# Layer 0's first four rows normed and turned two by two in all eight banks; angles at the beginning; first two pieces by halves in turns

## The reference, cut to what matters

```python
def rms_norm(x, g):
    y = x * lax.rsqrt(jnp.mean(x * x, axis=-1, keepdims=True) + NORM_EPS)
    return y * g

def partial_rope(x, pos):                 # the first 16 of 64 columns of each head
    inv = jnp.power(ROPE_THETA, -jnp.arange(half) / half)
    ang = pos[..., None] * inv
    x1, x2, rest = x[..., :half], x[..., half:ROT_DIM], x[..., ROT_DIM:]
    return concatenate([x1 * cos(ang) - x2 * sin(ang), x2 * cos(ang) + x1 * sin(ang), rest])

def swa_sink_mixer(h, pos, w_in, sinks):
    q, k, v, gate = split_cols(h @ w_in, [1024, 256, 256, 1024])
    q, k = partial_rope(q, pos), partial_rope(k, pos)
    o = banded_attention(q, k, v, SWA_WINDOW - 1, sinks)
    return o * silu(gate)

for i in range(2):
    x = x + mixer(rms_norm(x, norm)) @ w_out
return rms_norm(x, final_norm)
```

## Time and profile before

| | us |
|---|---|
| median of 3 runs | 1314.26 (1313.46 to 1314.52) |
| profiled execution, its own time | 1312.6 |
| its span | 1310.8 |
| PE busy | 1269.5 (97%) |
| DVE busy | 766.0 (58%) |
| ACT busy | 643.1 (49%) |
| POOL busy | 367.4 (28%) |

### The profile page before, as it was taken

One profiled execution on the slowest core, in us unless ns is written; L12 is line 12 of the kernel. 1 busy time (PEld: TensorE's weight loads), 2 busy tenths in 40 slices (PEclk: granted clock), 3 DMA queues, 4 the chain that ended last, 5 costly groups with the idle time before them and its releaser, 6 DMA issues. The chain is left out here.

```text
span 1310.8 us, 24577 instructions
## 1 busy us (share of the span) xinstructions
PE 1269.5 (97%) x8714; PEld 1183.4 (90%) x8714; DVE 766.0 (58%) x2339; ACT 643.1 (49%) x1777; POOL 367.4 (28%) x427
## 2 busy tenths in 40 slices
PE   4999999999899999999999999999999999998997
PEld 4998998988699999999989999899999899987997
DVE  5745453554672545666546766556765476767925
ACT  6444454454651444554446554446554455545312
POOL 2312142240301022212214932216832118611010
PEclk9999999999999999999999999999999999999999
DMA  5101012031545201110112211202310213215623
GB/s 201 38 20 50 26 54 84 18 98 38 173 146 201 97 25 53 39 26 20 53 53 67 84 57 36 65 28 81 107 34 19 65 40 100 76 27 154 192 99 129
DMA packets 101224, 97.29 MB, mean 74 GB/s; under 512 B 30705, under 2 KB 87537, under 8 KB 101105
## 3 DMA queue, kind: packets, MB, share of 16 engines
q1 hardware_dynamic: 101104, 95.73, 24.5%
HBM read 79.46 MB, written 16.25 MB: 73 GB/s over the span
## 5 line engine op out<-in xcount | busy, mean ns | idle before, releaser
L1161 PE MATMUL j_bank<-w_hi,ht_hi 128*128 128x384 f32 (+1 forms) x1312 | 445.4, 339 | 6.3 <-ACT v L1417 2.4
L1161 PE MATMUL j_bank<-w_lo,ht_hi 128*128 128x384 f32 (+1 forms) x1312 | 433.2, 330 | 0.0
L1161 PE MATMUL j_bank<-w_hi,ht_lo 128*128 128x384 f32 (+1 forms) x1312 | 433.1, 330 | 0.0
L1161 PEld LDWEIGHTS j_bank<-w_hi,ht_hi 128*128 128x128 f32 x1312 | 248.8, 190 | 18.8 <-issue 12.2
L1056 POOL TENSOR_TENSOR w_lo<-w_raw,w_hi 128x768 fp32r<-128x768 f32 (+1 forms) x60 | 103.2, 1720 | 558.6 <-ACT w_hi L1394 510.3
L1403 ACT ACTIVATE probs<-probs,stat 128x256 f32<-128x256 f32 (+1 forms) x512 | 231.2, 454 | 49.1 <-DVE stat L1661 47.5
L1161 PEld LDWEIGHTS j_bank<-w_lo,ht_hi 128*128 128x128 f32 x1312 | 249.1, 190 | 0.0
L1161 PEld LDWEIGHTS j_bank<-w_hi,ht_lo 128*128 128x128 f32 x1312 | 248.7, 190 | 0.0
L792 ACT COPY probs_t<-t_bank 128x256 f32<-128x256 f32 (+1 forms) x128 | 58.0, 453 | 289.4 <-PE o_bank L1304 283.7
L1394 ACT ACTIVATE w_hi<-w_raw 128x768 fp32r<-128x768 f32 (+1 forms) x120 | 88.6, 765 | 82.0 <-PE j_bank L1161 43.3
L1653 DVE CUSTOM_DVE_ANT_0 probs<-s_bank,masks 128x256 f32<-128x256 f32 x224 | 86.2, 421 | 54.2 <-PE t_bank L1283 53.5
(11 more groups left out here) (170 smaller groups left out, 1853.0 us busy)
## 6 DMA issues: line engine op xcount, KB each, us to landing
w_raw<-in_w_qkv SPq DMA_DIRECT2D x64, 384.0 KB, 3.4
coef<-coef_dram SPq DMA_DIRECT2D x96, 128.0 KB, 2.9
w_raw<-in_w_gate SPq DMA_DIRECT2D x32, 256.0 KB, 3.4
mix_dram<-xr SPq DMA_DIRECT2D x12, 512.0 KB, 3.9
w_raw<-in_w_out SPq DMA_DIRECT2D x16, 384.0 KB, 3.8
qk<-mix_dram SPq DMA_DIRECT2D x12, 512.0 KB, 4.2
xr<-in_x SPq DMA_DIRECT2D x8, 512.0 KB, 7.6
out<-xr SPq DMA_DIRECT2D x7, 512.0 KB, 2.7
```

The source lines that it names most:

```text
L1161: last = pe.matmul(to, a(x_, kt), b(y_, kt), start=(start and kt == kts[0] and x_ == y_), stop=(stop and kt == kts[-1] and x_ == 1))
```

## The change

The first four rows are squared one by one on ACT as they land. Rows 0 and 1 have their own `inverse` (on semaphores `first_v`, `first_a`) and are scaled on DVE; rows 2 and 3 have a second one and are scaled by DVE in columns 0 to 511 and by ACT in 512 to 1023. PE turns row 0 for all `kt`, then row 1, then rows 2 and 3 `kt` by `kt`, into eight banks at once (`first_bank`: both `j_bank`, both `t_bank` and the four of `norm_bank`). ACT calls a tiny square root first of all. Its two splits of quarters 2 and 3 stand together behind `kt` 4. PE then does half of piece 0, half of piece 1, the other half of 0, the other half of 1. The turns of rows 4 to 7 stand behind pieces 2 and 3, four `kt` each. The positions are loaded by ACT's DMA queue on their own semaphore; ACT's first `empty_norm` now waits for 32 of `small_in` (gain and sinks). `rope_angles` is cut in three: cast, products and first reduction come first of all on DVE, the second reduction stands at k = 2, and `rope_tables` moves from k = 4 to k = 3.

```diff
-NORM_BEHIND = {1: (0, 1, 2), 2: (3, 4, 5), 3: (6, 7)}
+NORM_BEHIND = [{2: (0, 1, 2, 3), 3: (4, 5, 6, 7)}, {1: (0, 1, 2), 2: (3, 4, 5), 3: (6, 7)}]
...
+        first_bank = [j_bank[PIECE.bank(("qkv", 0, 0))], j_bank[PIECE.bank(("qkv", 0, 1))], t_bank[0], t_bank[1]] + norm_bank
...
-            sp.dma_start(pos_i[:, :, :], positions).then_inc(small_in, 16)
...
+            def norm_first():
+
+                for b, e in ((0, "v"), (1, "v")):
+                    pe.wait_ge(xn_done[e], b + 1)
+                    for kt in range(KT):
+                        pe.transpose(first_bank[kt][:, b * P:(b + 1) * P], xr[:, b, kt * P:(kt + 1) * P], ident[:, :])
+                for kt in range(KT):
+                    if kt == 0:
+                        pe.wait_ge(xn_done["v"], 3)
+                    if kt == 4:
+                        pe.wait_ge(xn_done["a"], 1)
+                    for b in (2, 3):
+                        last = pe.transpose(first_bank[kt][:, b * P:(b + 1) * P], xr[:, b, kt * P:(kt + 1) * P], ident[:, :])
+                    last.then_inc(norm_full, 1)
...
             pe.wait_ge(consts, 1)
-            for kt in range(6):
-                norm_piece(0, kt, 0)
+            norm_first()
             piece(("qkv", 0, 0), (0,))
-            for kt in range(6, KT):
-                norm_piece(0, kt, 0)
+            piece(("qkv", 0, 1), (0,))
...
-                            piece(item[1:], (1,) if layer == 0 and k == 0 else (0, 1))
-                    for kt in NORM_BEHIND.get(k, ()):
+                            piece(item[1:], (1,) if layer == 0 and k < 2 else (0, 1))
+                    for kt in NORM_BEHIND[layer].get(k, ()):
...
+            act.dma_start(pos_i[:, :, :], positions).then_inc(pos_in, 16)
...
                 if layer == 0 and i == 0:
-                    act.wait_ge(small_in, 48)
+                    act.wait_ge(small_in, 32)
...
-            norm_half(0, 0, [(0, 0)])
-            w_hi([(0, 1)])
+            def square_first(n):
+
+                act.wait_ge(x_in[n], 16)
+                if n > 0:
+                    act.wait_ge(squared["va"[n % 2]], (n + 1) // 2)
+                act.activation(square_a, xr[:, n, :], ACT.Square, accum_out=sums[:, n:n + 1]).then_inc(squared["av"[n % 2]], 1)
...
+            act.activation(sums[:, NB:NB + 1], no_sink[:, 0:1], ACT.Sqrt, scale=0.0)
+            square_first(0)
+            square_first(1)
+            act.wait_ge(first_v, 1)
+            act.activation(ssq[:, 1, 0:2], ssq[:, 0, 0:2], ACT.Sqrt).then_inc(first_a, 1)
+            square_first(2)
+            square_first(3)
+            act.wait_ge(norm_v, 1)
+            act.activation(ssq[:, 1, 2:4], ssq[:, 0, 2:4], ACT.Sqrt).then_inc(norm_a, 1)
+            w_hi([(0, 0), (0, 1)])
+            act.wait_ge(norm_v, NORM_LINKS)
+            for n in (2, 3):
+                last = act.activation(xr[:, n, 512:], xr[:, n, 512:], ACT.Copy, scale=ssq[:, 2, n:n + 1])
+            last.then_inc(xn_done["a"], 1)
             for kt in range(KT):
                 empty_norm(0, kt, 0)
-                if kt == 3 or kt == 5:
-                    w_hi([(0, 2 if kt == 3 else 3)])
+                if kt == 4:
+                    w_hi([(0, 2), (0, 3)])
             norm_half(0, 1)
             w_hi(splits_of("start, next job"))
...
-            norm_half(0, 0)
+            angles()
+            less_turns(0, 2 * np.pi * 256)
+            dve.wait_ge(squared["a"], 1)
+            dve.wait_ge(squared["v"], 1)
+            inverse(0, slice(0, 2), first_v, first_a)
+            for n in (0, 1):
+                dve.tensor_scalar(xr[:, n, :], xr[:, n, :], ssq[:, 2, n:n + 1], None, ALU.mult).then_inc(xn_done["v"], 1)
+            dve.wait_ge(squared["a"], 2)
+            dve.wait_ge(squared["v"], 2)
+            inverse(0, slice(2, 4))
+            for n in (2, 3):
+                last = dve.tensor_scalar(xr[:, n, 0:512], xr[:, n, 0:512], ssq[:, 2, n:n + 1], None, ALU.mult)
+            last.then_inc(xn_done["v"], 1)
             w_lo(splits_of("start"))
             for kt in range(KT):
                 empty_norm(0, kt, 0)
-                if kt == 3:
+                if kt == 4:
                     w_lo(splits_of("start, second half"))
             norm_half(0, 1)
...
                     if layer == 0 and k == 2:
-                        rope_angles()
+                        less_turns(1, 2 * np.pi)
+                        within_half_turn()
+                    if layer == 0 and k == 3:
+                        rope_tables()
                     if layer == 0 and k == 4:
-                        rope_tables()
                         constants()
```

More of the change, by code:

```diff
@@ L523, in trunk, with bank_of_norm @@
         norm_bank = [s_bank[0], s_bank[1], o_bank[0], o_bank[1]]
+        first_bank = [j_bank[PIECE.bank(("qkv", 0, 0))], j_bank[PIECE.bank(("qkv", 0, 1))], t_bank[0], t_bank[1]] + norm_bank
+        def bank_of_norm(layer, kt, half):
+            return first_bank[kt] if layer == 0 and half == 0 else norm_bank[(KT * half + kt) % 4]
         def gate_of(layer, g):
@@ L1146, in norm_piece @@
                     pe.wait_ge(norm_empty["v"], 2 * KT * layer + i - 3)
-                elif layer == 1:
+                else:
                     pe.wait_ge(spare_empty, len(SPARE))
@@ L1150, in norm_piece @@
                     for e in "av":
-                        pe.wait_ge(xn_done[e], 4 * layer + 2 * half + 2)
+                        pe.wait_ge(xn_done[e], 4 * layer + 2 * half + (1 if e == "a" else 3))
                 for b in range(4):
@@ L1428, in empty_norm @@
                 if layer == 0 and i == 0:
-                    act.wait_ge(small_in, 48)
+                    act.wait_ge(small_in, 32)
                 if layer == 1 and kt == 0:
                     act.wait_ge(piece_full, PIECE.filled(("out", 0, OUT_PARTS - 1, 4 * half + 3)))
-                act.activation(ht[0][:, kt, half * 512:(half + 1) * 512], norm_bank[i % 4][:, :], ACT.Copy,
+                act.activation(ht[0][:, kt, half * 512:(half + 1) * 512], bank_of_norm(layer, kt, half)[:, :], ACT.Copy,
                                scale=gain[:, layer, kt:kt + 1]).then_inc(norm_empty["a"], 1)
@@ L1697, in empty_norm @@
                 dve.wait_ge(norm_empty["a"], 2 * KT * layer + i + 1)
[L1698 removed]
+                dve.scalar_tensor_tensor(out=ht[1][:, kt, cols], in0=bank_of_norm(layer, kt, half)[:, :],
                                          scalar=gain[:, layer, kt:kt + 1], in1=ht[0][:, kt, cols].bitcast(F32),
@@ L1845, in inverse_final, with inverse @@
                 inverse(4 + part, slice(*FINAL_ROWS[part]))
-            def inverse(index, blocks):
+            def inverse(index, blocks, done=norm_v, rooted=norm_a):
                 base = NORM_LINKS * index
                 var, y, z = ssq[:, 0, blocks], ssq[:, 2, blocks], ssq[:, 3, blocks]
[L1851 to L1857, removed]
+                link(dve.tensor_scalar(var, sums[:, blocks], 1.0 / D, EPS, ALU.mult, ALU.add), done, base + 1)
+                dve.wait_ge(rooted, index + 1)
+                link(dve.reciprocal(y, ssq[:, 1, blocks]), done, base + 2)
+                link(dve.tensor_tensor(z, y, y, ALU.mult), done, base + 3)
+                link(dve.tensor_tensor(z, z, var, ALU.mult), done, base + 4)
+                link(dve.tensor_scalar(z, z, -0.5, 1.5, ALU.mult, ALU.add), done, base + 5)
+                link(dve.tensor_tensor(y, y, z, ALU.mult), done, base + 6)
             def scale_rows(layer, half):
@@ L1896, in constants @@
             def constants():
+                dve.wait_ge(small_in, 32)
                 dve.tensor_scalar(neg_sink[:, :], sink[:, :], -1.0, None, ALU.mult).then_inc(sink_neg, 1)
@@ L1911, in constants, with angles @@
                 link(dve.tensor_scalar(masks[:, 5, :], key_f, row_f[:, 0:1], MASKED, ALU.is_gt, ALU.mult), mask_v, 4)
[L1913 to L1926, removed]
+            ang = rope_w[:, 0, :].rearrange("p (t j) -> p t j", j=HALF_ROT)
+            def angles():
+                dve.wait_ge(pos_in, 16)
+                link(dve.tensor_copy(pos_f[:, :, :], pos_i[:, :, :]), rope_v, 1)
                 flat = gate[:, 0, 608:608 + 3 * NB]
@@ L1930, in rope_angles, with less_turns, within_half_turn @@
                     last = dve.tensor_scalar(ang[:, :, j], flat, freq, None, ALU.mult)
-                chain(last)
+                link(last, rope_v, 2)
+            def less_turns(n, period):
+                turns, part = rope_w[:, 1, :], rope_w[:, 2, :]
                 magic = 1.5 * 2.0 ** 23
[L1933 to L1944, removed]
+                rest, parts = period, []
+                for bits in (9, 9):
+                    unit = 2.0 ** (np.floor(np.log2(rest)) - bits + 1)
+                    parts.append(np.floor(rest / unit) * unit)
+                    rest -= parts[-1]
+                parts.append(rest)
+                done = 2 + 8 * n
```

(8 more changed lines are left out.)

4 lines of the change are left out of this document (added).

## The result

| | before | after |
|---|---|---|
| median, us | 1313.47 (12 runs, 1311.94 to 1314.52) | 1315.05 (12 runs, 1313.76 to 1317.90) |
| ratio after / before | | 1.0016, 95% interval 1.0009 to 1.0024 |
| profiled execution, us | 1312.6 (span 1310.8) | 1313.8 (span 1312.0) |

The change makes the kernel slower by 1.6 us between the medians, 2.1 us by the ratio (1.2 to 3.2). The forecast was +2.2, with a time of 1316.5. Of the 1.4 us between that and 1315.05, 0.8 lies in the kernel before, whose median over 12 runs is 1313.47 and not 1314.26.

The account below looks back on a forecast made before the run. PE was taken to bound the kernel, its start settled by the wait ending at 33.10. Gains of 0.9, turns of 1.35 and a clock fall of 1.8 gave +2.2 us: 1316.5, range 1313.9 to 1317.7.

Parts of the forecast that it names:

- Rows as they land: First x rows: squared and scaled on landing, so PE can begin at 10.0 instead of 14.64.
- S: Moment of ACT's first emptying of a turned bank, 16.95 before; forecast 16.7, leaving 0.25 us of PE's earlier start.
- All eight banks: ACT's emptying of turned banks: no waits for PE between tiles, DVE done at S + 7.0, saving 0.6 us.
- The wait: PE before piece 2: idle 5.2 us until ACT empties piece 0's bank at 32.2, replacing a wait of 1.36.
- The turns: Twelve turns of rows 4 to 7, formerly done while PE waited, now follow piece 2: 1.35 us on the path.
- The clock: PE's clock falls to half around the wait before piece 2, costing 1.8 us (1.6 to 2.3); chance 0.55.
- Angles: DVE's 3.65 us of angle work moved to the start, tables to k = 3: hidden, no stall, no gain.
- rival 2: At the start: S is set by the turns, not the sinks, at 14.1, everything 2.6 us earlier, sum -2.2; chance 0.04.

Follow-up runs that it names:

- x1: The changed kernel with ACT's emptying of piece 0 moved ahead of its root, between the squares of rows 4 and 6; ratio to before 0.9970, 3.9 us less.
- x7: The kernel before with only the turns of rows 4 to 7 moved behind pieces 2 and 3; ratio to before 1.0022, +2.9 us.
- x2: The changed kernel with 45 needless turns on PE ahead of piece 2, in place of its wait; ratio to before 1.0001.
- x8: The changed kernel with all angle work back at k = 2 on DVE and the tables at k = 4; ratio to before 1.0017.
- x9: The changed kernel with the gain on its own semaphore and ACT's first emptying waiting for that alone, not the sinks; ratio to before 1.0019, +2.5 us.
- x5: The kernel before with the positions on ACT's DMA queue and own semaphore, ACT's first emptying waiting for gain and sinks alone; ratio 0.9989, -1.4 us.
- x10: The changed kernel with the edits of x1 and x9, and quarters 2 and 3 split behind tile 7 on ACT and DVE; ratio to before 0.9969, -4.1 us.

## Why the prediction was right

By its own steps:

- *Rows as they land.* PE's first turn at 9.86 (10.0 forecast).
- *S.* Taken as 16.7 with ends 16.1 and 16.95; 16.08 in the profiled execution, 16.08 to 16.92 over five. The saving was put at 0.25 and was 0.87 in this pair, since the loads of this execution landed early.
- *All eight banks.* DVE free at S + 7.07 (S + 7.0); the chain behind it 8.42 (8.44).
- *The wait.* 4.93 us of idle time from 26.7 to 31.6 (5.2 from 27.0 to 32.2), released by ACT's v copy, as forecast. x1, which takes it away, is 6 us faster than the changed kernel, three times the loss: the wait hid what the rest of the start had gained.
- *The turns.* 1.35 forecast, 1.3 in the rows; x7 has 2.81 more than the kernel before from piece 2 to the score, close to 1.35 and the loss of 3.4 us at half clock, 1.6.
- *The clock.* The fall came, and cost 2.2 where 1.8 was taken (inside the 1.6 to 2.3 given). x2 measured 1.8 with a start 0.4 later, so 2.2 as well. That it would come was given 0.55 and no firm order was found beforehand, so this step was a guess that the rows leaned to; without it the sum stood at +0.4. The Trainium skill's advice of no idle gaps above about 3 us ("TensorE: Matmul & The Clock Gate", "Why this matters for your kernels") held at this place in each case tried: in this start, idle times of 2.78, 3.21, 3.29, 4.93, 4.94, 5.38 and 5.40 were followed by low clock, and x8's front pause of 2.64 was not. Elsewhere it did not hold: 3.39 us of idle time before 338.61 in the kernel before, and the clock stayed up.
- *Angles.* No stall, nothing gained (x8).

The time of +2.2 came from terms of which two were off in opposite directions: S by -0.6 in this execution, the clock by +0.4. That they nearly cancel is luck. What was wrong though it did no harm is rival 2: it priced an S of 14.1 at a gain of 2.6 us. x9 had S = 14.27 and gained nothing that the runs can tell, because the second weight quarters were next in line. I had dismissed them with landing times near 18 and 19 against needs at 19.5 and 20.3, which holds for S = 16.7 alone. Also not foreseen: DVE's w_lo at 12.59 took 2.57 and not 0.95, with POOL's running beside it.

## What to carry to other kernels

An engine's earlier start is worth what the last wait before its unbroken run lets through: follow the releaser of that wait back through the program order of its engine before moving anything else. Here the releaser was a copy that stood some 6 us behind the moment at which it could have run, and moving it in the changed kernel gave 6.0 us, 3.9 against the kernel before. Work that fills a wait is free, and moving it behind the wait costs it twice, once for the work and once for a clock that falls when nothing is left to do.

## What the runs showed of the hardware that was not expected

- The clock can fall after the engine is back at work: 1.7 us after in x1, 0.6 in x7. A fall within a long wait costs what is left of the low stretch behind it (4.8 us of work in the changed kernel, 5.8 in x8). A wait of 3.39 us at 335 in the kernel before was not followed by a fall, and one of 2.52 in the changed kernel was (340.20), so idle time alone does not order these cases.
- Behind the start, ten of the twelve profiled executions have one to three more low stretches of 3.4 us, about 1.6 us lost in each (an estimate at 0.46 for each us low). All but one begin inside a pause of PE's or at most 1.2 us behind it: a pause of 2.4 to 3.5 us near 335 to 342, of 1.80 at 351, or of 1.30 near 1205. The same pauses pass without a fall in other executions. x2's and x5's had no such stretch: granted 1.00 from 16.5 to 1300 and from 20 to 1300.
- PE begins at the slow pace, 0.216 us a turn, and got to the fast one, 0.109, with nothing but turns to do. In x1 that was at 13.0, having begun at 10.30; in the changed kernel at 15.9, having begun at 9.86. The starts are the same.
- 8 KB of sinks (64 bytes sent to each of 128 partitions) delayed ACT's first square from 4.90 to 6.62 when issued ahead of x, and took 5.6 us to landing; the positions' 12 KB in the same place took 1.8 and delayed nothing.
- DVE's subtraction of 768 columns took 2.57 us at 12.59, with POOL's running from 12.24 to 14.34, and 0.95 at 13.68 before, where POOL's began at 15.36. In all nine executions with the changed start POOL's began 0.3 us ahead and DVE's took 2.57 or 2.58, ending 0.8 behind POOL's. In x10 a square of DVE's took 2.60 and not 1.22, at 22.57, with POOL's running until 24.08. All this fits a DVE that stands until POOL's instruction ends. No run took them apart, so the cause is not shown.
